# In two of the six gate-up places, the last contraction tile of an expert's weights is loaded as 119 and 9 partitions

## What is computed

```python
def hier_moe(h, w_group, b_group, w_router, b_router, w_gate, w_up, w_down):
    x = h.reshape(-1, D_MODEL)
    ...
    comb = (jax.nn.one_hot(g_idx, N_GROUPS, dtype=jnp.float32)[:, :, None]
            * (g_gate[:, None] * w_e)[:, None, :]).astype(x.dtype)
    y = jnp.zeros_like(x)
    for g in range(N_GROUPS):
        a = jnp.einsum('td,edf->tef', x, w_gate[g])
        u = jnp.einsum('td,edf->tef', x, w_up[g])
        hid = jax.nn.silu(a) * u * comb[:, g, :, None]
        y = y + jnp.einsum('tef,efd->td', hid, w_down[g])
    return y.reshape(h.shape)
```

## Time and profile before

| | us |
|---|---|
| median of 3 runs | 1625.04 |
| lowest, highest | 1620.2, 1628.69 |
| profiled execution, its own time | 1623.64 |
| its span, first to last instruction | 1621.8 |

### The profile page before, as it was taken

One profiled execution on the slowest core, in us unless ns is written; L12 is line 12 of the kernel. 1 busy time (PEld: TensorE's weight loads), 2 busy tenths in 40 slices (PEclk: granted clock), 3 DMA queues, 4 the chain that ended last, 5 costly groups with the idle time before them and its releaser, 6 DMA issues. The chain is left out here.

```text
span 1621.8 us, 24084 instructions
## 1 busy us (share of the span) xinstructions
PE 1270.1 (78%) x8176; PEld 899.3 (55%) x8176; DVE 642.7 (40%) x1579; ACT 432.4 (27%) x971; POOL 259.0 (16%) x366
## 2 busy tenths in 40 slices
PE   6988889997945997777078899999798289878740
PEld 4777778876843544443045677767576255434420
DVE  4455553335543332222533344344364523222218
ACT  3555554443020110001111244444420211101110
POOL 1111122220112232112310000000001223211124
PEclk9898899997966998899579999999889589999985
DMA  4211223405149999996710000000031799999943
GB/s 158 68 61 55 94 63 122 178 16 187 44 177 339 388 374 381 384 375 248 288 44 17 14 15 15 27 14 14 30 119 45 321 323 370 364 374 378 395 176 118
DMA packets 61380, 290.80 MB, mean 179 GB/s; under 512 B 12688, under 2 KB 23120, under 8 KB 44256
## 3 DMA queue, kind: packets, MB, share of 16 engines
q1 hardware_dynamic: 50720, 270.62, 44.7%
q0 software_dynamic: 10560, 18.90, 3.7%
HBM read 275.91 MB, written 29.29 MB: 188 GB/s over the span
## 5 line engine op out<-in xcount | busy, mean ns | idle before, releaser
L1779 PE MATMUL psum<-w_gu,moe_experts_xgT 128*64 128x256 f32 x1968 | 266.0, 417 | 72.1 <-DMA w_gu<-in_w_gate_up 55.2
L1779 PEld LDWEIGHTS psum<-w_gu,moe_experts_xgT 128*64 128x64 f32 x1968 | 152.7, 148 | 174.5 <-issue 126.2
L197 PE MATMUL psum<-x_hi,ab_w_hi 128*128 128x288 f32 x384 | 126.3, 329 | 4.3 <-DVE ab_k_tok L855 3.2
L1822 ACT ACTIVATE moe_experts_silu<-psum 64x256 f32<-64x256 f32 x64 | 24.2, 378 | 370.5 <-PE psum L1779 354.3
L198 PE MATMUL psum<-x_lo,ab_w_hi 128*128 128x288 f32 x384 | 116.1, 302 | 0.0
L199 PE MATMUL psum<-x_hi,ab_w_lo 128*128 128x288 f32 x384 | 116.0, 302 | 0.0
L1842 DVE COPY moe_experts_xgT<-psum 128x512 f32<-128x512 f32 x64 | 44.3, 692 | 179.1 <-PE psum L1769 179.0
L1733 POOL DMA_INDIRECT y_d<-mix,moe_slots x60 | 55.2, 920 | 371.3 <-DVE mix L1855 366.9
L1796 PE MATMUL psum<-w_dn,moe_experts_hidT 128*64 128x512 f32 x352 | 85.1, 604 | 2.2 <-issue 2.2
L1850 DVE COPY moe_experts_hidT<-psum 128x128 f32<-128x128 f32 x64 | 18.7, 292 | 167.2 <-PE psum L1787 156.5
L197 PEld LDWEIGHTS psum<-x_hi,ab_w_hi 128*128 128x128 f32 x384 | 75.4, 196 | 12.9 <-issue 12.3
(11 more groups left out here) (295 smaller groups left out, 2336.6 us busy)
## 6 DMA issues: line engine op xcount, KB each, us to landing
w_gu<-in_w_gate_up SPq DMA_DIRECT2D x54, 2048.0 KB, 36.3
w_dn<-in_w_down SPq DMA_DIRECT2D x44, 1024.0 KB
xT<-in_w_down SPq DMA_DIRECT2D x20, 1024.0 KB, 38.0
w_gu<-in_w_gate_up SPq DMA_DIRECT2D x10, 1536.0 KB
w_gu<-in_w_out SPq DMA_DIRECT2D x4, 2048.0 KB, 17.7
w_gu<-y_d SPq DMA_DIRECT2D x16, 512.0 KB, 7.4
xT<-in_w_gate_up SPq DMA_DIRECT2D x10, 512.0 KB
xT<-cum_d SPq DMA_DIRECT2D x8, 544.0 KB, 7.0
```

What stands on the lines that cost most here:

```text
L197: nc.tensor.matmul(dst, r32(ah), r32(bh), start=first, stop=False)
L1779: last = nc.tensor.matmul(gu(s)[h * CB:(h + 1) * CB, 0:EH], xgT[:, s, j, :], gate_up_tile(k.w_gu[n], j)[:, h * EH:(h + 1) * EH], start=(j ...
L1822: nc.scalar.activation(silu[:, s, :], gu(s)[0:CB, 0:EH], ACT.Silu).then_inc(silu_ready, 1)
```

## The change

`load_gate_up` gets the number of its place. For places 0 and 3 (`LEANING`) it loads seven of the eight tiles as before, in one DMA, and the eighth in two: partitions 0 to 118 and partitions 119 to 127. The bytes and where they go are the same. PE's wait counts 48 per load in these places in place of 16 (`pieces`). The other places, the down matrices and all other stages stay.

```diff
+LEANING = (0, 3)
+
+
+def pieces(parts, n):
+
+    return len(parts) + (2 if n in LEANING else 0)
+
+
+def load_gate_up(k, sp, layer, expert, gu_in, parts, n):
 ...
     for part in parts:
-        wide = part.shape[1] * 2 * EH
-        sp.dma_start(part.rearrange("p j n -> p (j n)"), row[:, at:at + wide]).then_inc(gu_in, 16)
-        at += wide
+        tiles = part.shape[1] - (1 if n in LEANING else 0)
+        sp.dma_start(part[:, 0:tiles, :].rearrange("p j n -> p (j n)"), row[:, at:at + tiles * 2 * EH]).then_inc(gu_in, 16)
+        if n in LEANING:
+            for lo, hi in ((0, 119), (119, P)):
+                sp.dma_start(part[lo:hi, tiles, :], row[lo:hi, at + tiles * 2 * EH:]).then_inc(gu_in, 16)
+        at += tiles * 2 * EH
...
-                        hold(pe, passed, (gu_in[n], 16 * len(k.w_gu[n]) * held), (xgT_ready, b + 1), *since(hid_ready, b - 1))
+                        hold(pe, passed, (gu_in[n], 16 * pieces(k.w_gu[n], n) * held), (xgT_ready, b + 1), *since(hid_ready, b - 1))
```

More of the change, by code:

```diff
@@ L1144, in _ @@
                 copy_k(NT - 1)
-def load_gate_up(k, sp, layer, expert, gu_in, parts):
+LEANING = (0, 3)
+def pieces(parts, n):
+    return len(parts) + (2 if n in LEANING else 0)
+def load_gate_up(k, sp, layer, expert, gu_in, parts, n):
     row, at = k.w_gate_up[layer, bass.ds(expert, 1)].rearrange("a p n -> p (a n)"), 0
     for part in parts:
-        wide = part.shape[1] * 2 * EH
-        sp.dma_start(part.rearrange("p j n -> p (j n)"), row[:, at:at + wide]).then_inc(gu_in, 16)
-        at += wide
+        tiles = part.shape[1] - (1 if n in LEANING else 0)
[4 more added lines that the diff above has]
+        at += tiles * 2 * EH
 def gate_up_tile(parts, j):
@@ L1177, in prefetch_gate_up @@
     for n in slots:
-        load_gate_up(k, sp, layer, n, k.gu_in[layer][n], k.w_gu[n])
+        load_gate_up(k, sp, layer, n, k.gu_in[layer][n], k.w_gu[n], n)
 def prefetch_down(k, sp, layer, slots):
@@ L1681, in _ @@
                     sp.wait_ge(gu_used[n], b // DEEP)
-                    load_gate_up(k, sp, layer, b, gu_in[n], k.w_gu[n])
+                    load_gate_up(k, sp, layer, b, gu_in[n], k.w_gu[n], n)
                     if b > DEEP:
@@ L1695, in _ @@
                         hold(sp, passed, (gu_used[n], held - 1))
-                        load_gate_up(k, sp, layer, expert[s], gu_in[n], k.w_gu[n])
+                        load_gate_up(k, sp, layer, expert[s], gu_in[n], k.w_gu[n], n)
                     for s in range(TRIP):
```

## The result

The kernel after took 1671.89 us (median of 4 runs, 1662.03 to 1676.49), the kernel before 1623.0 us (4 runs, 1620.2 to 1628.69). The ratio is 1.0289, 95% interval 1.0233 to 1.0344: 49 us slower. The forecast was 1643.4 with a range up to 1652. The side was right, the size was not: 18 us were foreseen. The profiled execution of after is the fastest of its four (1662.03, span 1660.2), so its rows explain 38 us.

What follows compares the result with a forecast made beforehand. The prediction took the expert weight stream through the DMA engines as the bound. Nine loads per layer at 1.02 us on seven engines gave 18.4 us in both layers; 1625.0 + 18.4 = 1643.4 us, range 1624 to 1652.

Steps and rivals of the forecast that it cites:

- Bytes and bound: Expert stages of both layers: bytes unchanged, and the weight stream through the never-resting DMA engines sets their length.
- (2), the deal: Divided eighth tile: 119 rows go to seven engines, 17 each, and nine rows to nine engines, one each.
- (2), late engines among the seven: End of each expert stage: a latest engine is among the seven, about three in four, making the full 9.2 us count.
- (2), the price of a row: Divided eighth tile: a 2 KB row costs an engine 101 ns, from 21 ns plus 0.0389 ns per byte.
- (2), "the nine others lose 0.64 us": Per divided load, the nine other engines carry 0.64 us less of big rows, two of them taking back 0.10.
- (2), the surplus: Saturated expert stages: seven engines gain 1.02 us per divided load, nine loads 9.2 us per layer, 18.4 in both.
- (3), SP: SP issues 22 more DMAs per layer; the backlog covers 0.8 us more per divided load, so no cost.
- (4), PE: PE waits for 48 per load on the same semaphore; waits lengthen only through the slower loads, nothing is added.
- A: Rival, late engines relieved: they are among the nine that get less; at best 3 us gained per layer, 1619; chance 0.11.
- B: Rival, the deal stays even: 119 rows go by eights over 15 engines, 2.3 us per layer, 1630; chance 0.13.
- C: Rival, only the overshoot counts: late engines are not among the seven; +8 us, 1633; chance 0.11.
- D: Rival, the queue blocks: SP is stopped earlier, nine engines run dry, 1 us more per load, 1662; chance 0.05.

Runs made afterwards that it cites:

- e6: Kernel after, with a block's tokens filling the slots from 63 down instead of from 0 up: 1655.75 us, ratio 1.0199 to the kernel before.
- e7: Kernel before, with a block's tokens filling the slots from 63 down instead of from 0 up: 1627.99 us, ratio 1.003.
- e1: Kernel after, but the eighth tile of places 0 and 3 is one undivided DMA of 128 partitions: 1623.94 us, ratio 1.0003 to the kernel before.
- e13: Kernel after, but the eighth tile is divided by columns into two DMAs of 128 partitions, 1 KB rows: 1626.92 us, ratio 1.0014 to before.
- e11: Kernel after, with the filled slots turned by four per block: 1649.81 us, ratio 1.0165 to the kernel before.
- e8: Kernel before, with the filled slots turned by four per block: 1611.41 us, ratio 0.9911.
- e4: Kernel after, but the eighth tile is divided as 115 and 13 partitions: 1678.5 us, ratio 1.0333 to the kernel before.
- e2: Kernel after, but the eighth tile is divided evenly, as 112 and 16 partitions: 1643.2 us, ratio 1.0124 to the kernel before.
- e14: Kernel before, with whole 16 KB-row gate-up loads of places 0 and 3 divided into partitions 0 to 63 and 64 to 127: 1873.8 us, ratio 1.1561.
- e15: Kernel before, plus HBM-to-HBM copies of the eighth tile of blocks 6, 9, ... 27 as 112 and 16 rows: 1628.56 us, ratio 1.0029.
- e16: Kernel before, plus HBM-to-HBM copies of the eighth tile of blocks 6, 9, ... 27, each one DMA of 128 rows: 1627.85 us, ratio 1.0027.
- e5: Kernel before, plus HBM-to-HBM copies of seven gapless 20,480 B rows behind blocks 6, 9, ... 27: 1626.69 us, ratio 1.0018.
- e9: Kernel before, plus HBM-to-HBM copies of seven 20,480 B rows, 1,024 B apart, behind blocks 6, 9, ... 27: 1632.3 us, ratio 1.0052.

## Why the prediction was wrong

**Bytes and bound: right.** The stream is the bound; PE's waits for gate-up loads grew by 43.2 us, from 55.2 to 98.4, and the span by 38.4.

**(2), the deal: right.** The prediction took it as an assumption. 119 rows go to seven engines, nine to nine, by the counts of 4-byte packets (16 per leaning load), and the shares of block 31's load land as nine within 1.2 us and seven that start 8.7 us later.

**(2), late engines among the seven: right**, by the landings, e6 and e7. It was put at three in four and came true. One reading beside it was off: the tail of before goes on to 765 us (0.08 in the window behind the earlier trace rows), so the mean engine ends some 12 us before the last one, not 7. Seven engines of mean lateness, 9.2 us heavier, would have ended before today's last and not 2 us after it.

**(2), the price of a row: close.** 101 ns were taken for a 2 KB row from the two queues' means; undivided (e1) such rows take 101 ns on average, in after 122.

**(2), "the nine others lose 0.64 us": here the step failed.** The sum added the seven's extra rows to engines that otherwise kept the pace of the earlier trace rows, some 378 GB/s; it has no term for a slower pace. The runs show that a load divided by partitions slows the packets of the whole stream while it is in flight. That has nothing to do with the surplus: 20 us for 112 + 16, 31 us for 64 + 64, 250 us when the large rows are divided, nothing to be measured for e1 and e13. The term, some 20 of the 49 us, is missing from the sum, and no row of before could give it, since that kernel has no load divided like this in its stream. None of the forecast's bounds or rivals allowed for a change of pace.

**(2), the surplus: right in kind, too small.** 18.4 us were forecast. From 112 + 16 to 119 + 9 the runs show 28.7, with an uncertainty of some 10 us from the two intervals. By rows of after: seven engines have 18 rows in place of the 8 of an even deal, 10 x 122 ns x 9 loads x 2 layers = 22 us, most of it. How much of it is paid depends on which engines are late. The whole change costs 49 us as it stands, 38 with the slots turned in both kernels (e11 less e8) and 28 with them reversed (e6 less e7), so 10 to 20 us of it are there only because the late engines are among the seven.

**(3), SP: right.** e1 and e13 issue 22 and 44 DMAs more and stay within 0.1 and 0.2%, so the issues cost nothing. SP's waits for PE fell from 54.8 us to 36.9, still a backlog:

```profile
SPq L1163 <- PE psum L1792: 36.9, 6, 18.2
```

**(4), PE: right**, as far as the traces show; its waits are for the loads.

**The signs.** A longer tail, by some 9 us: seen, but 25 us in place of 20. A share under 1.00 before 740 us: hardly, 0.98 in one window of five, then 0.90 from 740 to 760; the loss of pace doesn't show in the share at all, only in the GB/s. The hardware queue's share up by 0.2%: no, by 1.3%, which is the missing term.

**The rivals.** A fell with e6 and e7. B fell with the packet counts. C fell with e6, since the late ones are among the seven. D, the queue that blocks, gave the nearest number (1662). Its mechanism is there, but only for moments. An issue of SP that begins at 745.19 is held up for 8.25 us, and meanwhile the share falls to 7/16:

```profile
751.00:754.00 3.00, 3.00 (x24) 1.71 (x22) 0.28 (x1) 0.28 (x1) 0.00 (x0) 0.75 0.44 179
```

Nine engines at rest and seven at work make this share. The same happens around 689 us (an issue of 9.99 us, a share of 0.47 from 689 to 690), and in e4, where five engines are loaded, the share is 0.31, or 5/16, from 696 to 700 us, while an issue takes 12.86 us. But the seven stay fed, as the prediction held against D, and they set the end; e2 pays its 20 us without any such rest before 760 us. None of the rivals was that the packets themselves get slower, though the earlier trace rows showed 378 GB/s as the figure on which the whole sum stood; a rival that moves it by 5% would have given 25 us.

**Open** are: why 64 + 64 keeps its small rows in flight longer than 112 + 16; which slots of an indirect DMA an engine gets; and what exactly the packets wait for on the chip's side.

## What to carry to other kernels

Where a weight stream is the bound, keep every load in it at all 128 partitions, and if one must be split, split it by columns (1.001), never by partitions (1.012 to 1.156 here, even when every engine gets the same share). When a stream slows, compare GB/s at equal busy share before counting packets. And look at how the shares of one load land: here two of sixteen came late with the filled rows of the indirect DMAs, and spreading those rows gained 12 us.

## What the hardware showed that was not expected

- Loads divided by partitions slow other DMAs' packets: the mean 16 KB packet of the stage takes 667 ns in before, 679 with the tile undivided (e1), 716 divided (after), 1,037 with the large rows divided (e14), while copies within HBM with the same division cost nothing (e15 against e16, 0.7 us).
- A contiguous copy within HBM of seven rows of 20,480 B is dealt in 16 shares (e5: 16 packets of 8,960 B and 16 of 4 B per DMA), and in seven only when the rows lie apart (e9: seven of 20,480 B and seven of 4 B).
- Which slots of the indirect DMAs are filled decides whether engines are late. With always the first 36 of 64 filled, two of the 16 shares of a load land some 7 us behind the rest; turning the slots from block to block removes that and gains 12 us over the two layers (e8).
- When a few engines have much more queued than the others, SP is held up in an issue (8.25 us in after, 12.86 in e4) and the others run dry: the share stands at 0.44 (7/16) in after and at 0.31 (5/16) in e4 for some us.
- Lateness follows the filled rows: two of 16 shares are late in before and none when the slots are turned (e8), and with the slots reversed the kernel after gains 16 us while the kernel before loses 4.5 (e6, e7).
